# Modulation as per-feature columns applied at eviction, and adaLN groups 1 and 5 multiplied by TensorE

## What is computed

```python
mod = silu(c) @ ada_w[l] + ada_b[l]                 # six vectors of 1024 for each layer
sh_a, sc_a, g_a, sh_f, sc_f, g_f = split(mod, 6)
h = x * (1 + sc_a) + sh_a                           # modulate, before the projections
y = attention(h @ w_in) @ w_o
x = layer_norm(ALPHA * x + (1 + g_a) * y) * ln_g + ln_b
h = x * (1 + sc_f) + sh_f
m = grouped_moe(h)                                  # router, top 2 of 16, gate/up/down per expert
x = layer_norm(ALPHA * x + (1 + g_f) * m) * ln_g + ln_b
```

## Time and profile before

| | us |
|---|---|
| median of 3 runs | 1028.05 (1027.62 to 1033.05) |
| the profiled execution, its time | 1031.61 |
| its span, first to last instruction | 1029.9 |
| from the span's start to layer 0's first projection | 41.0 |
| first projection to the first fox head | 91.2 |
| fox heads | 58.5 |
| output product of layer 0 | 33.0 |
| output product to the first expert of layer 0 | 47.0 |
| experts of layer 0 | 248.3 |
| experts to layer 1's first projection | 17.7 |
| layer 1's projections | 92.2 |
| differential heads and their transposes | 43.8 |
| output product of layer 1 | 35.3 |
| output product to the first expert of layer 1 | 46.7 |
| experts of layer 1 | 262.0 |
| last norm and store | 13.3 |

### The profile page before, as it was taken

The page is one execution under the profiler, slowest core; times in us unless marked ns, Lnnn a source line. Parts: engine busy times, 40 slices in busy tenths (PEclk is TensorE's granted clock), DMA queues, the critical chain, the costliest instruction groups (busy, mean ns, idle before and its releaser), DMA issues.

```text
span 1029.9 us, 11402 instructions
## 1 busy us (share of the span) xinstructions
PE 930.8 (90%) x3734; PEld 454.2 (44%) x3735; DVE 378.5 (37%) x818; ACT 203.2 (20%) x422; POOL 163.4 (16%) x171
## 2 busy tenths in 40 slices
PE   4899999979899999799989998697989988989996
PEld 1487445436433333233348475544633333323332
DVE  2476745745111111111176478633511111111114
ACT  0000133211122111212211004610212122122211
POOL 3085400000400000000054071300050000000000
PEclk9899999997999999899989999888899999999999
DMA  9989969640199999679982978104039999987911
GB/s 322 383 314 387 376 234 375 276 164 0 32 430 428 428 428 429 270 299 429 408 331 84 377 273 329 81 1 163 0 123 428 428 428 430 430 343 328 430 56 41
DMA packets 63864, 296.48 MB, mean 288 GB/s; under 512 B 5804, under 2 KB 5932, under 8 KB 51544
## 3 DMA queue, kind: packets, MB, share of 16 engines
q1 hardware_dynamic: 61200, 295.71, 71.8%
q10 hardware_dynamic: 2632, 0.36, 0.2%
HBM read 295.01 MB, written 1.05 MB: 287 GB/s over the span
## 4 chain that ended last, share of the span: by engine, by line
PE 80%; DVE 10%; DMA 4%; issue 3%; ACTq 2%; ACT 1%; POOL 1%; POOLq 0%; SPq 0%; DVEq 0%
PE ps L1475 22%; PE ps L1486 11%; PE ps L1345 11%; PE ps L1493 7%; PE ps L1421 5%; PE ps L1360 5%; PE ps L1467 3%; DMA ring<-in_moe_w_up_dram 2%; DMA ring<-in_moe_w_down_dram 2%; PE ps L1301 2%; PE ps L1251 1%; PE ps L1437 1%; PE ps L1372 1%; PE ps L1546 1%; DVE h L845 1%
## 5 line engine op out<-in xcount | busy, mean ns | idle before, releaser
L1475 PE MATMUL ps<-ring,hT 128*64 128x512 f32 x560 | 255.4, 608 | 18.2 <-issue 11.1
L1476 PE MATMUL ps<-ring,hT 128*64 128x512 f32 x560 | 255.8, 608 | 0.0
L1475 PEld LDWEIGHTS ps<-ring,hT 128*64 128x64 f32 x560 | 75.5, 139 | 175.4 <-issue 173.4
L1486 PE MATMUL ps<-ring,arena 128*64 128x512 f32 x280 | 130.5, 610 | 9.0 <-DMA ring<-in_moe_w_down_dram 5.8
L1487 PE MATMUL ps<-ring,arena 128*64 128x512 f32 x280 | 130.5, 610 | 0.0
L1345 PE MATMUL ps<-hT,ring 128*128 128x256 f32 x512 | 113.8, 385 | 2.3 <-ACT hT L621 1.7
L1068 DVE TENSOR_TENSOR arena<-arena,ps 128x256 f32<-128x256 f32 x32 | 13.5, 421 | 265.4 <-ACT arena L717 156.4
L1345 PEld LDWEIGHTS ps<-hT,ring 128*128 128x128 f32 x512 | 98.6, 193 | 18.1 <-issue 2.3
L554 POOL COPY hT<-arena 128x512 f32 x32 | 19.6, 613 | 464.9 <-PE ps L1476 289.5
L367 DVE SCALAR_TENSOR_TENSOR arena<-ring,csig,arena 128x512 f32<-128x512 f32 x84 | 82.6, 983 | 3.0
L1493 PE MATMUL ps<-arena 128*128 128x512 f32 (+1 forms) x168 | 77.7, 605 | 4.2 <-DVE arena L1096 2.4
(11 more groups left out here) (268 smaller groups left out, 997.2 us busy)
## 6 DMA issues: line engine op xcount, KB each, us to landing
ring<-in_moe_w_gate_dram SPq DMA_DIRECT2D x32, 2048.0 KB, 14.0
ring<-in_moe_w_up_dram SPq DMA_DIRECT2D x32, 2048.0 KB, 18.4
ring<-in_moe_w_down_dram SPq DMA_DIRECT2D x32, 2048.0 KB, 16.3
ring<-in_ada_w_dram SPq DMA_DIRECT2D x24, 2048.0 KB, 14.7
ring<-in_fox_w_in_dram SPq DMA_DIRECT2D x6, 2048.0 KB, 13.7
ring<-in_kv_ada_w_dram SPq DMA_DIRECT2D x4, 2048.0 KB, 13.4
ring<-in_kv_w_dram SPq DMA_DIRECT2D x4, 2048.0 KB, 17.6
ring<-in_fox_w_o_dram SPq DMA_DIRECT2D x2, 2048.0 KB, 20.3
```

The costliest lines, as they stand in the source:

```text
L1475: mg = t.matmul(ps[0:CAP, bank, :], lhs(k), wcols(ng)[:, k, :], start=(k == 0), stop=(k == KC - 1))
L1476: mu = t.matmul(ps[CAP:P, bank, :], lhs(k), wcols(nu)[:, k, :], start=(k == 0), stop=(k == KC - 1))
L1486: t.matmul(ps[0:CAP, bank, :], lhs(f), wdown(n)[:, f, 0:512], start=(f == 0), stop=(f == 3))
```

## The change

**Columns, not rows.** The modulation is kept with one feature to a partition (`modc`, a gain and an offset for each of eight feature blocks). After the layer norm VectorE writes only the normalised stream; it is transposed as it is, and the gain and offset are applied while it is read out of PSUM (`modulated`: an activation with scale and bias on ScalarE, a tensor_scalar on VectorE). The same stands for the expert gather. `spread_fold`, `spread_norm`, `streamed` and `fold_rows` are gone; the summed rows are turned into columns by four transposes (`turn_mod`). The layer norm's own rows and the gates' biases come by DMA (`lnw`, `gbc`). One transposition of the stream serves both K/V and W_q, whose modulated copy goes to `hcols` (the space of `h`). The first stream comes transposed from DRAM (`x_t`).

**Groups 1 and 5** are multiplied by TensorE (`mod_product(1)` after unit 12, `mod_product(5)` between V and W_q). Groups 2 and 6 are summed by VectorE alone, four pieces each; GpSimd sums nothing.

**Also:** the layer norm's variance comes from `bn_stats`/`bn_aggr` on halves; the router multiplies 32-column weights in four strips of the array, then adds them by a second small product; some of the routing's small steps are gone; GpSimd reads both window starts before it waits for the gathered tokens; all weights are laid out on the host so that each partition of a piece is one run of 16 KB (before, a column piece was eight runs of 2 KB; expert matrices had one run already).

```diff
-        SUMS = {1: 1, 2: 2, 5: 3, 6: 4}
+        SUMS = {2: 1, 6: 2}
...
             def mod_product(gi):
...
-                if gi == 3:
-                    pe.wait_ge(mod_row, 2)
+                if gi in (3, 5):
+                    pe.wait_ge(mod_row, gi - 1)
+                if gi == 5:
+                    for s_ in range(2):
+                        pe.wait_ge(ht_ready[s_], HT_N[3])
                 for n in ns:
                     landed(pe, n)
...
-            def norm_sums(norm, b):
+            def norm_sums(norm, b, s_):
+                half = slice(512 * s_, 512 * s_ + 512)
+                link(d.tensor_tensor(h[:, b, half], gbc[:, norm % 2, half], ps[:, 2 * b + s_, :], ALU.mult))
+                link(d.scalar_tensor_tensor(out=xres[:, b, half], in0=xres[:, b, half], scalar=ALPHA, in1=h[:, b, half],
+                                            op0=ALU.mult, op1=ALU.add))
+                link(d.bn_stats(bst[:, b, s_, :], xres[:, b, half]))
...
             def turned(m):
+                norm = M_NORM[m]
                 for b in range(NB):
-                    dve.wait_ge(ht_mm, NB * m + b + 1)
-                    d.tensor_copy(hT[:, 4:8, b * P:(b + 1) * P],
-                                  ps[:, turn_bank(m) + 2 * b + 1, :].rearrange("p (k s) -> p k s", k=4)).then_inc(ht_ready[1], 1)
+                    dve.wait_ge(ht_mm, 4 * norm + 2 * b + 2)
+                    for k in range(4, KC):
+                        modulated(hT[:, k, b * P:(b + 1) * P], turned_bank(b, k), m, k).then_inc(ht_ready[1], 1)
...
             def route(l):
+                stream_turned(m)
+                for kk in range(2):
+                    for strip in range(4):
+                        k = 4 * kk + strip
+                        mm = t.matmul(ps[32 * strip:32 * strip + 32, 0, 0:S], rw[:, k, :], hT[:, k, :],
+                                      start=(kk == 0), stop=(kk == 1))
+                mm.then_inc(rt_mm, 1)
+                zeroed((2, 3))
+                pe.wait_ge(lt_r, l + 1)
...
+            turn_mod(1, 4)
+            spread_gate(0, 5)
             natural_units(u + 1, N_FOXV)
...
-            u = turned_units(UNITS0, N_KVK)
-            pe.wait_ge(h_ready, 2 * 4)
-            spread_norm(1)
+            u = turned_units(UNITS0, N_KVK, hT)
             u = natural_units(u, N_KVV)
-            pe.wait_ge(x_ready, NB * 2)
-            mod_sum(5)
-            pe.wait_ge(mod_row, 5)
-            turn_stream(3)
+            mod_product(5)
             stream_turned(3)
-            turned_units(u, N_WQ)
+            for piece in N_WQ:
+                u = turned_units(u, [piece], hcols)
+                if piece == N_WQ[0]:
+                    turn_mod(5, 4)
+                    spread_gate(2, 5)
             mod_sum(6)
```

More of the change, by code:

```diff
@@ L440, in load @@
                     spent(sp, n - RING)
-                sp.dma_start(wpiece(n), pieces[n]).then_inc(full[slot(n)], 16)
-            def wpiece(n):
-                return wcols(n) if len(pieces[n].shape) == 3 else ring[:, slot(n), :]
+                sp.dma_start(ring[:, slot(n), :], pieces[n]).then_inc(full[slot(n)], 16)
             def expert_loads(l):
@@ new lines, in first_turned @@
+            def first_turned(half):
+                act.wait_ge(x_in, 16)
+                act.wait_ge(cols_r, half + 1)
+                for k in range(4 * half, 4 * half + 4, 2):
+                    modulated(hT[:, k, :], hcols[:, k, :], 0, k).then_inc(ht_ready[0], 1)
+            for half in range(2):
+                spent(act, N_ADA[0][2 * half])
+                a.activation(parts[:, 2 * half, :], ps[:, 2 * half, :], ACT.Copy).then_inc(part_ev[0], 1)
+                first_turned(half)
@@ new lines, in first_cols @@
+            def first_cols(half):
+                lo = 4 * half
+                for which, (gi, v_) in enumerate((SC[0], SH[0])):
+                    at = 2 * half + which
+                    dve.wait_ge(col_mm, at + 1)
+                    ins = d.tensor_tensor(modc[:, 0, which, lo:lo + 4], ps[:, 4 + at, 0:4],
+                                          ada_cols(gi, v_)[:, lo:lo + 4], ALU.add)
+                    if which:
+                        ins.then_inc(cols_r, 1)
+                        dve.wait_ge(cols_r, half + 1)
+                    else:
+                        link(ins)
@@ new lines, in post_norm @@
+                finish = last_normed if norm == 3 else normed
+                if norm == 3:
+                    dve.wait_ge(lw_in, 32 * (norm + 1))
+                for s_ in range(2):
+                    y_ready(norm, 0, s_)
+                    norm_sums(norm, 0, s_)
+                norm_stats(norm, 0)
+                y_ready(norm, 1, 0)
+                norm_sums(norm, 1, 0)
+                finish(norm, 0)
+                y_ready(norm, 1, 1)
+                norm_sums(norm, 1, 1)
+                norm_stats(norm, 1)
@@ L955, in rank4 @@
+                finish(norm, 1)
             def rank4(src, n, cmp, eq, dst):
@@ L1327, in stream_turned, with turn_mod @@
-            def stream_turned(m, b=NB - 1):
+                    pe.wait_ge(part_ev[at % 2], at // 2 + 1)
+                    for kk in range(4):
+                        mm = t.matmul(ps[:, 4 + at, kk:kk + 1], parts[:, at, kk * P:(kk + 1) * P],
+                                      strips[:, 0:1], start=True, stop=True)
+                    mm.then_inc(col_mm, 1)
+            def turn_mod(gi, bank):
+                pe.wait_ge(mod_row, gi)
+                for kk in range(4):
+                    mm = t.transpose(ps[:, bank, kk * P:(kk + 1) * P], mrow[:, MROW[gi], kk * P:(kk + 1) * P], ident[:, :])
+                mm.then_inc(mt_mm, 1)
@@ L1348, in turned_units @@
                         if u in after:
-                            mod_sum(after[u])
+                            mod_product(after[u])
                         u += 1
@@ L1413, in out_product @@
                 ns = N_WO[l]
-                norm = 2 * l
-                spread_gate(norm)
+                turn_mod((2, 6)[l], 4)
+                pe.wait_ge(mc_r, (3, 5)[l])
+                spread_gate(2 * l + 1, 5)
                 for n in ns:
```

729 lines of the change are left out of this document (354 added, 375 removed).

## The result

The changed kernel takes 1057.32 us (median of 4 runs, 1055.08 to 1059.44), the kernel before 1029.07 beside it. The ratio is 1.027, 95% interval 1.0235 to 1.0305: 2.7% slower. The profiled execution took 1059.44 with a span of 1057.7, so the two traces differ by 27.8 us.

| stage | before | after | moved | forecast |
|---|---|---|---|---|
| head, to the first projection | 41.0 | 37.0 | -4.1 | -7.5 |
| layer 0's projections | 91.2 | 102.4 | +11.2 | +10.8 |
| fox heads and output product 0 | 91.5 | 89.6 | -1.9 | -2.2 |
| to the first expert of layer 0 | 47.0 | 43.9 | -3.1 | -4.7 |
| experts of layer 0 | 248.3 | 244.9 | -3.4 | 0 |

The account below looks back on a forecast made before the run. TensorE was taken to bound the projections, loads the experts, VectorE's small steps and TensorE alternately the routing. Stage terms summed to +23.0 us, mainly layer 1's projections at +30.4, giving 1051 on the median; range 1034 to 1062.

Parts of the forecast that it names:

- Layer 1's projections, +30.4: K to the differential heads: product, load wait, cold starts and late VectorE sums make 122.6 us from 92.2.
- the stall: Between group 5's product and W_q 0 in layer 1: TensorE waits 18.1 us for the third load issued after the product.
- The sentence that nothing covers the load: In layer 1, W_q 0 directly follows group 5's product in TensorE's order, so its 18.1 us load wait is fully exposed.
- Layer 0's projections, +10.8: Layer 0: product of group 1 +6.0, turn and gate spread +2.2, waits for V pieces 1.7 and 0.9 us.
- Head, -7.5: Start to first projection: condition weights and a transposed stream let projections begin at 33.5 us, where they began at 41.0.
- Routing, -4.7 each: To the first expert, each layer: earlier routing, shorter small steps and earlier window starts outweigh a colder gather; 4.7 us less.
- Experts, 0: Experts of both layers: bound by their loads from first slot given back to last, so no change in time.
- Experts to K, +0.4: Between layer 0's experts and layer 1's projections: norm statistics by halves cost about 2 us, removed passes and spreads return most.
- Output product 1, -3.2: Layer 1's output product: old spreads go, a turn and gate spread come, as in layer 0; 3.2 us less.
- Last norm, +3.7: End of the kernel: eight passes by halves and four bn_stats on the ending path add 3.7 us.
- the covered loads: Rival, chance 0.08: W_q 0 in layer 1 has landed when the product ends; +2.8, 1031 us, no change.
- this rival: Rival, chance 0.12: TensorE's clock stays at 2.4 GHz through the new pauses; 17.3 us less, 1034.

Follow-up runs that it names:

- without the stall: The changed kernel with only its list of loads reordered, W_q's two loads ahead of group 5's and 6's: 1038.41 us, ratio 1.0097.
- the gate last: The changed kernel with VectorE taking group 5's columns and gate row after group 6's last sum: 1051.50 us, ratio 1.0206.
- the product ahead of V: The changed kernel with group 5's product between K and V, and its gate taken after group 6's last sum: 1036.76 us, ratio 1.0081.
- the sized filling: Groups 1 and 5 summed by VectorE, group 5's gate after group 6's sums, last norm as before, TensorE filling rows cut to the pauses: 1000.37 us, ratio 0.9713.

## Why the prediction held, point by point

The forecast was 1051, the median is 1057.3, inside the range of 1034 to 1062; the direction and the mechanism were right. The change costs 28.2 by the medians and 27.8 by the traces, for 23.0 in the sum. The sum is closer than its terms: stages that came out dearer than forecast missed by 10.9 together, those that came out cheaper (the experts, output product 1) by 6.2, and that these cancel in part is luck. Layer 1's projections, on which the verdict hangs, missed by 0.8.

- **Layer 1's projections, +30.4: 31.2.** Each term has its line above: K 30.57 (29.96 forecast), the product 7.00, the stall 17.89 (18.1), W_q 0 16.26 (16.04), turn and spread 2.17 (2.3), the sums' wait 5.17, with 0.84 inside W_q 1 for a unit's copy that stands behind a sum on VectorE (6.5 for both). The runs confirm both causes apart: 18.9 without the stall, 5.8 with the gate last. The sentence that nothing covers the load was the step on which it hung, and the product ahead of V shows what a cover does.
- **Layer 0's projections, +10.8: 11.2.** The waits for the two V pieces were 1.95 and 0.81, for 1.7 and 0.9:

```profile
109.58 14.00 PE L1373 MATMUL ps<-ring,hT 128*128 128x512 f32 x32 [1.95 <-DMA ring<-in_fox_w_in_dram]
124.39 14.00 PE L1373 MATMUL ps<-ring,hT 128*128 128x512 f32 x32 [0.81 <-DMA ring<-in_fox_w_in_dram]
```

- **Head, -7.5: -4.1.** The step that failed is "the fourth piece lands at about 25.9". It landed at about 28, since the transposed stream's 1 MB stood ahead of it in the queue, which I had left out (2.4 at 430 GB/s; my step of 4.9 a piece is 2 MB at the 429 of rows 1, not the 4.5 of rows 5 rounded). And not its landing set the last batch but the third batch: that one's piece landed at 22.95, and its 3.69 at half clock, the eviction and 1.87 of narrow products held TensorE until 29.21. What follows the start of the last batch took 7.8, for 7.6 in the sum. In the traces where the clock comes up early the head ends at 33.2 to 33.6, near the 33.5, but with the last batch begun at 28.1 and warm: that this meets my number is chance.
- **Routing, -4.7 each: -3.1.** Term by term in layer 0: routing starts 2.4 earlier (3.1 forecast), the small steps 1.1 shorter (1.5), the window starts 2.0 as forecast, the gather 16.61 for 14.14, 2.5 dearer (2.1). All four have the right sign; three miss, by 0.4 to 0.7.
- **Experts, 0: -3.4 in layer 0.** That the loads bind from the first slot on was right; the time up to the first slot was not looked at. Before, the first expert began 3.8 behind the gather (3.0 of it idle) and TensorE ran at a mean 0.82 of full clock up to 280; now it begins 1.8 behind it and runs at 1.00. The first slot comes back 7.2 after the first expert's start, not 8.9. So 1.7 of the 2.5 that the cold gather cost came back there: the cold start had in the main changed its place. The other 1.7 fell between the overflow pair's wait and the norm, 93.5 before and 91.8 after, and is not explained.
- **Experts to K, +0.4: +2.1.** The norm is 1.4 longer up to its last transposes. Four `bn_stats` of 0.70 (0.75 forecast, of 0.4 to 1.23) stand in it; I gave back too much for the two passes that went.
- **Output product 1, -3.2: -5.4 with the heads.** The two spreads of layer 1 had cost 3.78 and 3.43; the first ran cold, for which layer 0's 1.98 was no measure. Part of this is luck: the spread that came in their place ran at full clock in this execution, and in six of the thirteen traces it did not.
- **Last norm, +3.7: +4.8**, with GpSimd's power in the open (1.31 + 0.62 beside a pass), which my list of passes left out.

Of the rivals, the covered loads are out. Dear statistics are out at 0.70; the loads ran at 430 GB/s in these stages, as in the experts, so the old rate of 385 is best explained by the eight short runs, though no run changes the layout alone. The clock did fall at the new pauses that the sum counts (K, W_q 0, the gathers), and did not at the waits of 1.95 and 0.81 ahead of the V pieces, whose 14.00 is the full-clock time. The 17.3 that this rival took off rests in part on 5.3 for each routing, whose working it shows only for the gather's 2.1. But the sized filling shows that its price was no fate: with four or five products in the pause the gather and K ran at full clock.

## What to carry to other kernels

When a step that gave buffers back one by one becomes one that gives them all back at its end, follow the queue of loads behind them: the cost is not the step's seven microseconds but the first load that the next step needs, counted in its place in the queue, and it can be cured there or by putting other work behind the step. When an engine's wait is put ahead of work that needs nothing from it, look at who waits for that work. And split a change before judging it: here the two products, with the queue and the order they brought, lost about 4%, and all the rest together gained some 1%.

## What the runs showed of the hardware

Behind a pause TensorE's next work began at a granted clock of 0.50 and took longer: W_q 0, behind 17.9 us, 2.0 more; K, behind 6.1, 2.7 (30.57 for 27.86); the product behind 3.85, 2.5 (9.61 for 7.07); the gather, behind a routing with pauses of 4.5 and 1.7, 2.5 to 2.6 (16.5 for 14.0). The first expert, behind 1.8, began at 1.00. Rows of filling products in the pauses brought back 2.5 in the gather, and paid where they ended before the data was there. A 128x512 float32 product took 0.87 us at full clock, as two instructions. `bn_stats` on 128x512 took 0.694 on average, GpSimd's add on one column 0.22 alone and 1.31 while VectorE ran a pass with two SBUF operands (1.28) beside it; this agrees with what the Trainium skill (SBUF — State Buffer, SBUF: two separate sides) says of the two locking each other out. Column pieces of one 16 KB run a partition moved at 430 GB/s, the last column of this row of the changed kernel (busy time by stretch, layer 0's projections), where eight runs of 2 KB had given 385 to 387 in two short stretches with the DMA engines as full:

```profile
102.00:125.00 23.00, 20.24 (x58) 8.72 (x57) 21.50 (x34) 4.46 (x6) 0.00 (x0) 1.00 1.01 430
```
